# A PEER encoder on one core: the dot products read the normalised rows from PSUM, the mixers share four banks

## The reference, cut to what matters

```
h += W_out [ norm(StickBreaking(q,k,v)) || norm(ChunkMLP(u,v)) ]    # "mixers", all from one projection of norm(h)
h += PEER(norm(h))
h += (p @ W_ple) * sigmoid(norm(h) @ W_gate + b_gate)

def peer_tokens(xb, w_q, sub_keys, u_tab, v_tab):    # 8 heads, 16 of 16384 experts each
    ...                                              # scores, two top 16, top 16 of 256 sums
    u_sel = jnp.take(u_tab, idx, axis=0)
    hid = jnp.einsum('td,thkd->thk', xb, u_sel).astype(jnp.float32)
    a = (g * jax.nn.gelu(hid, approximate=False)).astype(xb.dtype)
    return jnp.einsum('thk,thkd->td', a, jnp.take(v_tab, idx, axis=0))
```

## Time and profile before

| | us |
|---|---|
| median of 3 runs | 3759.86 |
| fastest, slowest run | 3746.72, 3762.76 |
| span of the profiled execution, first to last instruction | 3730.2 |
| the profiled execution's own time | not recorded; the three runs lie 16.5 to 32.6 above its span |
| DVE, PE, POOL busy | 2767.5, 2764.3, 2581.7 |
| first dot, last gather (start) | 182.0, 3684.0 |

### The profile page before, as it was taken

How to read it: one execution, slowest core, us unless ns; L and a number is a source line. 1 busy time by engine, 2 the same in 40 slices (tenths; PEclk the granted TensorE clock), 3 DMA queues, 4 the chain that set the end, 5 groups by cost and what they waited for, 6 DMA issues and landing times.

```text
span 3730.2 us, 27568 instructions
## 1 busy us (share of the span) xinstructions
PE 2764.3 (74%) x7340; PEld 1262.9 (34%) x7340; DVE 2767.5 (74%) x6501; ACT 863.5 (23%) x1543; POOL 2581.7 (69%) x2198
## 2 busy tenths in 40 slices
PE   8637768998777777877867779887877776655667
PEld 4413424454322223443422234453422222221222
DVE  0377796687888887677887977888888878766661
ACT  3413212652100003253100142553100012200012
POOL 0066666677678776677777777777787777777772
PEclk9778889998899988988899889988899998877789
DMA  5288998988899999999999999999999999999994
GB/s 196 98 306 315 370 345 332 348 309 324 316 335 334 365 369 403 401 371 366 374 349 364 368 374 390 383 329 362 348 339 349 345 367 365 409 353 353 351 367 137
DMA packets 329970, 1266.53 MB, mean 340 GB/s; under 512 B 37781, under 2 KB 38805, under 8 KB 323161
## 3 DMA queue, kind: packets, MB, share of 16 engines
q0 software_dynamic: 313344, 1140.99, 82.6%
q1 hardware_dynamic: 16472, 123.79, 8.4%
HBM read 1256.96 MB, written 6.82 MB: 339 GB/s over the span
## 4 chain that ended last, share of the span: by engine, by line
POOL 33%; PE 22%; DMA 17%; issue 14%; DVE 11%; ACT 2%; another core or an unknown queue 1%; DVEq 0%; ACTq 0%; SPq 0%; POOLq 0%
POOL urows L789 17%; POOL vrows L789 16%; PE experts L1433 10%; DMA urows<-in_peer_u,idx 9%; DMA vrows<-in_peer_v,idx 7%; PE bank L1406 6%; DVE urows L1162 3%; PE bank L1416 3%; DVE h L1199 1%; DVE diag L1188 1%; DMA vrows<-in_peer_v,idx_sam 1%; DVE work L1072 1%; DVE part L1138 0%; DVE work L1128 0%
## 5 line engine op out<-in xcount | busy, mean ns | idle before, releaser
L1433 PE MATMUL experts<-vrows,diag 128*128 128x512 f32 (+1 forms) x2896 | 1584.8, 687 | 790.3 <-DMA vrows<-in_peer_v,idx 464.4
L1162 DVE CUSTOM_DVE_ANT_0 urows<-urows,xn 128x1024 f32<-128x1024 f32 x1088 | 1325.4, 1221 | 548.9 <-DMA urows<-in_peer_u,idx 470.8
L789 POOL DMA_INDIRECT urows<-in_peer_u,idx x1024 | 1216.3, 1188 | 615.4 <-issue 286.4
L789 POOL DMA_INDIRECT vrows<-in_peer_v,idx x1024 | 1218.2, 1190 | 405.5 <-issue 279.1
L1433 PEld LDWEIGHTS experts<-vrows,diag 128*128 128x128 f32 (+1 forms) x2896 | 561.3, 209 | 1673.7 <-issue 1328.0
L1406 PE MATMUL bank<-weights,xT 128*128 128x512 f32 (+1 forms) x1280 | 575.6, 602 | 4.1 <-ACT xT L849 4.1
L1199 DVE SCALAR_TENSOR_TENSOR h<-vrows,amount,h 128x1024 f32<-128x1024 f32 x364 | 466.3, 1281 | 0.0
L1406 PEld LDWEIGHTS bank<-weights,xT 128*128 128x128 f32 (+1 forms) x1280 | 223.5, 178 | 331.8 <-issue 325.8
L840 ACT ACTIVATE work<-bank 128x256 f32<-128x256 f32 (+3 forms) x100 | 42.2, 424 | 976.7 <-PE bank L1604 464.4
L1416 PE MATMUL bank<-xT,weights 128*128 128x288 f32 (+2 forms) x896 | 197.6, 384 | 14.8 <-ACT xT L849 6.1
L1416 PEld LDWEIGHTS bank<-xT,weights 128*128 128x128 f32 x896 | 163.0, 208 | 52.8 <-issue 8.2
(11 more groups left out here) (139 smaller groups left out, 2364.1 us busy)
## 6 DMA issues: line engine op xcount, KB each, us to landing
weights<-in_w_in SPq DMA_DIRECT2D x20, 2048.0 KB
weights<-in_w_out SPq DMA_DIRECT2D x10, 2048.0 KB
weights<-in_w_peer_q SPq DMA_DIRECT2D x10, 2048.0 KB
urows<-in_peer_u,idx POOLq DMA_INDIRECT x1024
vrows<-in_peer_v,idx POOLq DMA_INDIRECT x1024
weights<-in_w_ple_gate SPq DMA_DIRECT2D x8, 2048.0 KB
weights<-in_w_ple SPq DMA_DIRECT2D x4, 1024.0 KB
weights<-in_sub_keysT SPq DMA_DIRECT2D x5, 512.0 KB
```

The costliest lines, as they stand in the source:

```text
L789: pool.indirect_dma_start(out=rows[:, where, :], out_offset=None, in_=table, in_offset=bass.IndirectOffsetOnAxis(ap=index, axis=0))\
L1162: dve.tensor_tensor_reduce(row, row, xn2[:, t, :], 1.0, 0.0, ALU.mult, ALU.add, hid[:, j % 2, k:k + 1]).then_inc(dotted.sem, 1)
L1433: last = pe.matmul(experts[c][0:ROWS[t], :], diag[:, (4 * j + q) % ND, k % QUARTER, 0:ROWS[t]], vrows[:, n % NV, 512 * c:512 * c + 512], s ...
```

## The change

The eight banks are given out anew. `att_out` joins the shared ones as a fourth, and two of the former five become one tile `query` of 128 x 1024. At the first step of each tile's first item DVE copies that tile's `xn2` into `query`, waits for the copy and then runs the dots, whose second input is `query` in place of `xn2`. The dots' other input and their output stay in SBUF.

Which bank a use takes is worked out before the program is built: of those free in an earlier stage, the one that has been free longest. Until the first dot all six are shared; from then on `query` is kept, and the bank of `att_out` is kept from a tile's first attP (or samP) to its attM. `take` waits for what was in the bank before, and the heads take their bank through it as well.

```diff
-NB = 5
-BANK = {u: n % NB for n, u in enumerate(USES)}
-TAKEN_BEFORE = {u: USES[n - NB] for n, u in enumerate(USES) if n >= NB}
+HEADS_BANK = 3
+QUERY_BANKS = (4, 5)
+def attention_banks():
+    out = {}
+    for n, s in enumerate(SCHEDULE):
+        if (s[0] == "attP" and s[3] == 0) or s[0] == "samP":
+            out[s[1], SAMPLE if s[0] == "samP" else s[2]] = n
+    return {x: (n, SCHEDULE.index(("attM",) + x)) for x, n in out.items()}
+def give_banks():
+    first_dot = next(n for n, s in enumerate(SCHEDULE) if s[0] == "peer")
...
+    for n, s in enumerate(SCHEDULE):
+        if n in takes:
+            assert free_since[HEADS_BANK] < n
+            give(takes[n], HEADS_BANK)
+        for u in bank_uses(s):
+            fit = [b for b in range(6) if free_since[b] < n
+                   and not (b in QUERY_BANKS and ends[u] >= first_dot)
+                   and not (b == HEADS_BANK and any(n <= y and x <= ends[u] for x, y in heads.values()))]
+            give(u, min(fit, key=lambda b: free_since[b]))
+    last = [next(u for u in reversed(USES) if bank[u] == b) for b in QUERY_BANKS]
+    return bank, before, last
+BANK, TAKEN_BEFORE, LAST_IN_QUERY = give_banks()
...
-        banks = [bank(f"bank{n}") for n in range(NB)]
+        banks = [bank(f"bank{n}") for n in range(3)]
         att_out = bank("att_out")
+        query = ctx.enter_context(nc.psum_tensor("query", [P, D], F32))
+        banks += [att_out, query[:, 0:512], query[:, 512:1024]]
...
+            def load_query(l, t, j):
+                dve.wait_ge(*normed.after((l, t, "ffn")))
+                if t == SAMPLE:
+                    dve.wait_ge(packed, PACKED * (l + 1))
+                if j:
+                    dve.wait_ge(*dotted.after((j - 1, TOPK - 1)))
+                else:
+                    for u in LAST_IN_QUERY:
+                        dve.wait_ge(*bank_read[RELEASED_BY[u]].after(u))
+                dve.tensor_copy(query[:, :], xn2[:, t, :]).then_inc(query_ready.sem, 1)
+                dve.wait_ge(*query_ready.after((l, t)))
...
-                if k == 0 and t == SAMPLE:
-                    dve.wait_ge(packed, PACKED * (l + 1))
+                if k == 0 and e == 0:
+                    load_query(l, t, j)
...
-                dve.tensor_tensor_reduce(row, row, xn2[:, t, :], 1.0, 0.0, ALU.mult, ALU.add,
+                dve.tensor_tensor_reduce(row, row, query[:, :], 1.0, 0.0, ALU.mult, ALU.add,
...
-                        n = MOVES.index((l, t))
-                        if n:
-                            pe.wait_ge(*att_moved.after(MOVES[n - 1]))
+                        take(("attO", l, t))
```

More of the change, by code:

```diff
@@ L406, with give @@
 RELEASED_IN = {u: n for n, s in enumerate(SCHEDULE) for who, u in releases(s)}
-assert all(RELEASED_IN[TAKEN_BEFORE[u]] < n for n, s in enumerate(SCHEDULE) for u in bank_uses(s)
-           if u in TAKEN_BEFORE and TAKEN_BEFORE[u][:len(s)] != s)
+HEADS_BANK = 3
[8 more added lines that the diff above has]
+    first_dot = next(n for n, s in enumerate(SCHEDULE) if s[0] == "peer")
+    heads = attention_banks()
+    takes = {n: ("attO",) + x for x, (n, _) in heads.items()}
+    ends = {("attO",) + x: n for x, (_, n) in heads.items()}
+    ends.update(RELEASED_IN)
+    bank, before, holder, free_since = {}, {}, {}, {b: -1 for b in range(6)}
+    def give(u, b):
+        bank[u] = b
+        if b in holder:
+            before[u] = holder[b]
+        holder[b] = u
+        free_since[b] = ends[u]
+    for n, s in enumerate(SCHEDULE):
[10 more added lines that the diff above has]
+BANK, TAKEN_BEFORE, LAST_IN_QUERY = give_banks()
 def weight_unit(s):
@@ L630, in encoder @@
         dotted = Signal(sem("dotted"), steps)
+        query_ready = Signal(sem("query_ready"), [(l, t) for l, t, e in ITEMS if e == 0])
         gelu_done = Signal(sem("gelu_done"), range(ITEM_COUNT))
@@ L1152, in dot @@
                     return
-                l, t, _ = ITEMS[j]
-                if k == 0 and t == SAMPLE:
-                    dve.wait_ge(packed, PACKED * (l + 1))
+                l, t, e = ITEMS[j]
+                if k == 0 and e == 0:
+                    load_query(l, t, j)
                 if k == 0 and j >= 2:
@@ L1359, in take @@
                     before = TAKEN_BEFORE[use]
-                    pe.wait_ge(*bank_read[RELEASED_BY[before]].after(before))
+                    if before[0] == "attO":
+                        pe.wait_ge(*att_moved.after(before[1:]))
+                    else:
+                        pe.wait_ge(*bank_read[RELEASED_BY[before]].after(before))
+                if use[0] == "attO":
+                    return att_out
                 return banks[BANK[use]]
@@ L1551, in _ @@
                     pe.wait_ge(*act_read.after(("v", l, SAMPLE)))
-                    pe.wait_ge(*att_moved.after((l, SAMPLE - 1)))
+                    take(("attO", l, SAMPLE))
                     for e in range(H):
```

## The result

| | before | after |
|---|---|---|
| median of 6 runs, us | 3758.77 | 3720.81 |
| fastest, slowest run, us | 3733.06, 3762.76 | 3701.74, 3727.37 |
| ratio to before, 95% interval | | 0.9894 [0.9865, 0.9923] |
| span of the profiled execution, us | 3730.2 | 3717.5 |

The kernel became faster by 38 us, 1.1%. The prediction said 3575 (3470 to 3700); the time lies 146 us above it and 21 us above the range's end.

What follows compares the result with a forecast made beforehand. The prediction took POOL as the bound, its gathers delayed by DVE instructions with two SBUF inputs. Gathers 193, dots +5, query copy -7, banks -6 gave 185 us off 3760: 3575 us, range 3470 to 3700.

Steps and rivals of the forecast that it cites:

- What holds a gather: On POOL: a gather starting during a DVE instruction with two SBUF inputs ends some 0.81 us after it; one PSUM input prevents this.
- third rival: At the gathers' issue: the change removes no delay, time stays 3760; chance 0.08.
- How much of it is the dots': Of 529 us excess in the gathers' issue, the dots cause about 340 us; some 185 us stay.
- the 65%: Dots' share of the gathers' excess: 69% by count x duration squared for random starts, lowered for short routing and norm instructions.
- potential / (potential + slack): Weight per stretch: removable POOL delay against that plus POOL's time waiting for buffers; weighted gains sum to 193 us, unweighted 289.
- The caps: Per-stretch limit on the gain: room left up to 409 GB/s of DMA and 95% busy of DVE or PE.
- The dots' own duration: On DVE: each dot loses 10 ns with a PSUM input, 11 us over 1088, 5 us gained.
- The query copy: On DVE: ten new copies from SBUF to PSUM, 1.2 us each, 13 us with waits, 7 us lost.
- The banks: On PE: fewer shared banks make 12 takes late by 17.6 us in sum; 6 us lost.
- last rival: On PE: 72 additional near takes each wait 3.7 us for ACT, 266 us in all, time 3841; chance 0.05.
- first rival: On DVE or PE: one is next at once, its fullest stretches already at the ceiling, net gain 88 us, time 3672; chance 0.20.

Runs made afterwards that it cites:

- e1: The changed kernel with the dots reading xn2 in SBUF again, query copy and new bank order kept: 3762.28 us, 1.0011 of the time before.
- the two orders: The changed kernel with 5 u and 6 v row buffers, planner weights altered: STAGE_WEIGHT 0.7 took 3720.48 us; STAGE_WEIGHT 2.2 with DVE_WEIGHT 1.8 took 3752.81 us.
- e12: The changed kernel with xn2 in three slots in place of five, and 6 u and 5 v row buffers in place of 4 and 5: 3772.30 us, 1.0019.

## Why the prediction was wrong, step by step

**What holds a gather: right for the dots.** Hardly any gather beside a dot is held any more, 7 of 690, and e1 brings the holds back by the one operand. The third rival (nothing is taken away) is excluded. Two points were too simple, and the trace of before shows both (own counts). "Wherever in it the gather started" does not hold at the edges: of the gathers beside dots none that started in the first 25 ns was held, and of the 112 that were not held 20 started in the first 45 ns and 92 in the last 200. And a second full SBUF tensor is not the only cause: all 9 gathers that started inside a TENSOR_SCALAR of 128x1024 with over 0.2 us of it left (`xs<-h,guess`, whose second input is one number per partition) were held as well, while none of 20 beside SCALAR_TENSOR_TENSOR with a bank as input was, and none of 22 beside FIND_INDEX8.

**How much of it is the dots': nearly right.** 340 us were to go and 304 went. The dots' own share was 372. Part of it moved: gathers, no longer stopped at the dot, now start beside what DVE runs next. The sum took starts at random times, and they are not: a gather held by a dot ends at a fixed time after it, so the next one started in the last 200 ns of the row add behind that dot, too late to be held. Before, 172 of the 335 gathers that started beside row adds did so, 139 of them right behind a held gather; after the change 46 of 296 did, 8 of them behind a held one. So the dots had shielded gathers from the row adds, and that the 65% came out so near owes something to luck. Beside row adds the excess rose from 87 to 145 us, beside diagonals from 17 to 51 (own counts). One such pair, POOL and then DVE:
```profile
3325.96 1.60 POOL L829 DMA_INDIRECT urows<-in_peer_u,idx  x1 [0.30 <-issue]
```
```profile
3325.47 1.28 DVE L1252 SCALAR_TENSOR_TENSOR h<-vrows,amount,h 128x1024 f32<-128x1024 f32 x1
```

**What POOL's time is worth: here it failed.** The step is "potential / (potential + slack)" for each stretch. It turned 340 us into 193, a price of 0.57 us for each us of POOL. Measured: 0.13 (e1 against the change). The weight asks how much POOL already waits and takes a stretch without such waits for one that POOL owns. Little waiting shows only that the others did not keep POOL waiting at its pace. It does not show that they would have gone faster with rows that come earlier. They hardly did: 284 of the 327 us of holding (e1 against the change) turned into POOL's waiting for their dots and adds. The chain's 33% for POOL was read in the same way, as what could be had.

**The caps** of 409 GB/s and of 95% busy were never reached: DVE stayed at 342 and 344 of 400 us in its two fullest stretches, PE at 351 and 358. The sign named for being right, 370 to 400 GB/s from 1000 on, did not come either: the six stretches there moved 345 to 383, and 347 to 382 before.

**The dots' own duration: right**, 1213 against 1221 ns, -8 where -10 was taken. The Trainium skill, "VectorE: DVE Perf Modes", section on the TRN2 errata, has the PSUM source dearer by 62 cycles at 0.96 GHz; this trace disagrees now at the full shape too, with the dot 8 ns shorter.

**The query copy: right**, 1.22 us ten times. **The banks: small, as predicted.** Late takes came to 28 us in 17 takes, not 17.6 in 12 (own count); all idle time of PE that ends with ACT went from 43 to 66 us. e1 bounds both steps together by 12 us against the 13 summed. The last rival (PE stalls) is excluded.

**The first rival was nearest**: its sign for itself, "a DVE that is no fuller than before while POOL waits for it", is what the profile after shows (DVE 74% in both, POOL's wait for its dots 164.2 and 294.4 us). Its time, 3672, was 49 us low all the same, for it only lowered the caps and kept the weight elsewhere.

**The range** ended at 3700 because no case in which the holds go priced POOL's time below 0.25. The trace of before allowed a lower one: nothing in it excludes that POOL's share of the chain passes to the others whole.

**What lies around the span** was taken as 30 us. The profiled execution after has 3719.23 us for a span of 3717.5, so 1.7 us lies around it. The profiled execution of before was then one at the fast end of its runs (the fastest is 3733.06); this does not bear on the gain.

**What is shown and what is not.** Shown: the dots' holds went, they turned into waits for buffers nearly whole, and neither the holds, nor the number of row buffers, nor the diagonals, nor half of DVE's dots, of PE's adds or of the rows' bytes is worth more than 2% by itself. Not shown is what sets the time in their place. One explanation is the fixed list, with each queue in order and each hand-over (rows, dot, GELU, amounts, diagonals, add; bank, ACT, bank) a little late in turn; the two orders support it. The other is the late signals, which appear with the change, in waits where the list asks for nothing from another engine. Both may act together. Open: which hand-over would have to move, and what delays the signals. Neither was isolated, and no order was found that turns POOL's free time into a shorter span.

## What to carry to other kernels

An engine's share of the chain, and its lack of slack, say how much it takes part, not what its time is worth. Before working on it, measure the price: lengthen the engine's work and see what the time does. First look in the trace whether the cycle grew: here an added instruction of 0.12 us vanished in a pause of 0.30 us, and its run priced nothing. In this kernel, with three queues in one fixed order at 60 to 75% busy each, 327 us less on one of them brought 44. And look at waits in which an engine needs only its own last signal: they should be short, and where they grow, neither the order nor the amount of work explains it.

## What was unexpected

- A dot of 128x1024 with one PSUM input takes 1213 ns and leaves the gathers' issue alone (0.94 us beside it); with both in SBUF it takes 1221 and holds it (1.70).
- With the holds gone, 42 waits of PE and DVE for their own last signal exceed 1 us (the longest 7.6 us), against 3 before.
- Less work on PE made its remaining work slower: clock 0.869 to 0.738, the same matmul 592 to 1057 ns in the median.
- Two more u buffers (e12, beside the three slots of `xn2`) cost 1.3% (0.9894 to 1.0019). POOL's waits moved from the dots to the adds of v rows: for PE's from 239.9 to 404.0 us, for DVE's from 29.5 to 166.7, for the dots from 294.4 to 46.5. Why that costs time was not tried.
